# A hybrid decoder layer on one core: two expert weight loads wait for the row gathers, router logits with three copies of the columns, identity products on TensorE

## The reference

```python
h2 = rms_norm(x, ln2_g[l]) * (1.0 + scale2) + shift2
x = x + gate2 * hierarchical_moe(h2, w_rg[l], b_rg[l], w_re[l], b_re[l], w1[l], w3[l], w2[l])

def hierarchical_moe(h, w_rg, b_rg, w_re, b_re, w1, w3, w2):      # cut
    p_group = jax.nn.softmax(ht @ w_rg + b_rg)
    pg_top, g_idx = lax.top_k(p_group, 1)
    e_logits = (ht @ w_re + b_re).reshape(T, N_GROUPS, EXPERTS_PER_GROUP)
    e_logits = jnp.take_along_axis(e_logits, g_idx[:, :, None], axis=1)[:, 0]
    pe_top, e_idx = lax.top_k(jax.nn.softmax(e_logits), 2)
    weights = pg_top * pe_top / jnp.sum(pe_top, axis=-1, keepdims=True)
    ...
    hid = jax.nn.silu(lax.ragged_dot(xs, w1, sizes)) * lax.ragged_dot(xs, w3, sizes)
    ys = lax.ragged_dot(hid, w2, sizes) * weights[order][:, None]
    out = jax.ops.segment_sum(ys, tok, num_segments=T)
```

## Time and profile before

| | |
|---|---|
| median of 3 runs | 1135.82 us (1133.02 to 1141.98) |
| the profiled execution, its own time | 1136.39 us |
| its span in the profile | 1134.6 us |
| TensorE busy | 1037.5 us (91%) |
| VectorE, ScalarE, GpSimd busy | 49%, 30%, 13% |
| read from HBM, over the span | 271.99 MB, 243 GB/s with the writes |

### The profile page before, as it was taken

How to read it: one execution, slowest core, us unless ns; L and a number is a source line. 1 busy time by engine, 2 the same in 40 slices (tenths; PEclk the granted TensorE clock), 3 DMA queues, 4 the chain that set the end, 5 groups by cost and what they waited for, 6 DMA issues and landing times.

```text
span 1134.6 us, 19418 instructions
## 1 busy us (share of the span) xinstructions
PE 1037.5 (91%) x8496; PEld 686.1 (60%) x8496; DVE 556.7 (49%) x883; ACT 335.2 (30%) x567; POOL 149.4 (13%) x168
## 2 busy tenths in 40 slices
PE   4799999899998889999996599999999998999998
PEld 3567799798995668878786234444444443444443
DVE  4548861534536857575565333333333332333334
ACT  6367753032326762322322011111111111111110
POOL 0000000360894430000000100000000000000000
PEclk9899999998989989999997599999999999999999
DMA  9431121000004046566648599999999999999993
GB/s 365 150 149 56 60 90 38 14 5 4 4 3 149 7 148 206 185 215 212 223 167 334 199 380 406 404 396 408 401 408 412 411 417 403 414 413 410 421 419 131
DMA packets 44917, 273.26 MB, mean 241 GB/s; under 512 B 7408, under 2 KB 7552, under 8 KB 31008
## 3 DMA queue, kind: packets, MB, share of 16 engines
q1 hardware_dynamic: 41168, 264.42, 59.2%
q0 software_dynamic: 2656, 4.28, 1.3%
q10 hardware_dynamic: 1008, 3.31, 0.7%
HBM read 271.99 MB, written 4.19 MB: 243 GB/s over the span
## 4 chain that ended last, share of the span: by engine, by line
PE 68%; DMA 20%; DVE 7%; ACT 3%; issue 2%; SPq 0%; ACTq 0%; DVEq 0%; POOLq 0%
PE banks L1543 26%; DMA w_qkv<-in_w 17%; PE banks L1978 13%; PE banks L1992 6%; PE banks L2012 2%; PE banks L1694 2%; DMA tokm<-in_w_ada 2%; PE banks L1971 1%; PE banks L1696 1%; PE banks L1709 1%; PE banks L2013 1%; PE banks L1836 1%; DMA picked<-h_table,slot_rows 1%; PE banks L1984 1%; PE banks L1922 1%
## 5 line engine op out<-in xcount | busy, mean ns | idle before, releaser
L1978 PE MATMUL banks<-w_ring,xT 128*64 128x512 f32 x336 | 147.8, 593 | 8.5 <-DMA w_ring<-in_w 4.3
L1471 DVE TENSOR_TENSOR hid<-banks,silu_a 64x512 f32<-64x512 f32 x32 | 22.2, 693 | 197.4 <-ACT silu_a L841 197.4
L1978 PEld LDWEIGHTS banks<-w_ring,xT 128*64 128x64 f32 x336 | 45.2, 137 | 103.2 <-issue 103.2
L841 ACT ACTIVATE silu_a<-banks 64x512 f32<-64x512 f32 x32 | 18.9, 591 | 276.0 <-PE banks L1979 276.0
L1459 DVE SCALAR_TENSOR_TENSOR mod<-banks,row_weight,mod 64x512 f32<-64x512 f32 x64 | 47.9, 748 | 93.2 <-PE banks L1992 92.2
L930 POOL DMA_INDIRECT picked<-h_table,slot_rows x32 | 30.2, 944 | 468.2 <-PE banks L1971 398.3
L1978 PE MATMUL banks<-w_ab,xT 128*64 128x512 f32 x176 | 81.8, 620 | 6.1 <-DMA w_tok<-in_w 5.3
L1465 DVE TENSOR_TENSOR x<-x,banks 128x512 f32<-128x512 f32 x120 | 77.1, 684 | 18.7 <-PE banks L2013 18.3
L1992 PE MATMUL banks<-w_ring,hidT 128*64 128x512 f32 x352 | 82.1, 609 | 1.0 <-ACT hidT L845 1.0
L1979 PE MATMUL banks<-w_tok,xT 128*64 128x512 f32 x176 | 81.9, 621 | 0.0
L1979 PE MATMUL banks<-w_ring,xT 128*64 128x512 f32 x176 | 77.6, 594 | 0.0
(11 more groups left out here) (368 smaller groups left out, 2359.3 us busy)
## 6 DMA issues: line engine op xcount, KB each, us to landing
w_ring<-in_w SPq DMA_DIRECT2D x54, 2048.0 KB, 32.6
w_tok<-in_w SPq DMA_DIRECT2D x21, 2048.0 KB, 35.1
w_ab<-in_w SPq DMA_DIRECT2D x11, 2048.0 KB, 30.2
w_qkv<-in_w SPq DMA_DIRECT2D x10, 2048.0 KB, 35.9
ada_buf<-in_w_ada SPq DMA_DIRECT2D x64, 256.0 KB, 3.5
tokm<-in_w_gate SPq DMA_DIRECT2D x3, 2048.0 KB, 14.0
ring<-in_w_mix SPq DMA_DIRECT2D x5, 1024.0 KB, 4.7
ring<-in_w_ada SPq DMA_DIRECT2D x2, 2048.0 KB, 14.2
```

The source lines that it names most:

```text
L1978: pe.matmul(bank[2][0:SLOTS, :], xT[:, b, k, :], w1[:, k, :], start=(k == 0), stop=(k == KT - 1))
```

## The change

Three edits. (1) On SyncE, w3 of expert 2, and with it w2 of expert 2 and all that stands behind, waits for the landing of the first two gathers instead of for the stores of h2 (the gathers themselves still wait for the stores). (2) Each logits product reads the 36 router columns three times, through a step of zero, and writes 108 columns; VectorE reads the first copy of each. (3) TensorE multiplies the identity by four copies of itself, 128x512 in float32, into bank 5, which nobody reads: once after the logits of tile 0, nine times before the wait for the picks, twice before the wait for the slots, five times before the wait for the first gather.

```diff
@@ load_w13 @@
                 if e == 2:
-                    sp.wait_ge(h2_stored, 16 * TT)
+                    for b in range(2):
+                        sp.wait_ge(rows_in[b], 16)
                     sp.wait_ge(h2t_mm, KT)
                 sp.dma_start(W3_IN[c], w3_src[e]).then_inc(w3_in[c], 16)
@@ vector @@
-            seq(dve.tensor_tensor(L, bank[0][:, 0:TT * NR].rearrange("p (t n) -> p t n", n=NR),
+            seq(dve.tensor_tensor(L, bank[0][:, 0:3 * TT * NR].rearrange("p (t c n) -> p t c n", t=TT, c=3)[:, :, 0, :],
                                   b_route.unsqueeze(1).to_broadcast([P, TT, NR]), ALU.add))
@@ tensor @@
+            thrice = bank[0][:, 0:3 * TT * NR].rearrange("p (t c n) -> p t c n", t=TT, c=3)
+
+            def keep_running(n):
+                for _ in range(n):
+                    pe.matmul(bank[5][:, :].rearrange("p (a n) -> p a n", a=4), ident, ident.unsqueeze(1).to_broadcast([P, 4, P]), start=True, stop=True)
...
-                    mm = pe.matmul(bank[0][:, NR * t:NR * t + NR], h2T[:, k, P * t:P * t + P], w_route[:, k, :], start=(k == 0), stop=(k == KT - 1))
+                    mm = pe.matmul(thrice[:, t, :, :], h2T[:, k, P * t:P * t + P], w_route[:, k, :].unsqueeze(1).to_broadcast([P, 3, NR]),
+                                   start=(k == 0), stop=(k == KT - 1))
...
             turn_h2(1)
             logits(0)
+            keep_running(1)
             turn_h2(2)
             logits(1)
             logits(2)
             turn_h2(3)
             logits(3).then_inc(logit_mm, 1)
+            keep_running(9)
             pe.wait_ge(picks_v, 1)
...
             mm.then_inc(rank_mm, 1)
+            keep_running(2)
...
             fill_table(bank[4][0:SLOTS, 0:2 * NEXP], values.rearrange("p j c n -> p j (c n)"))
+            keep_running(5)
```

## The result

The changed kernel takes 1132.02 us (median of 20 runs, 1126.61 to 1135.42), the kernel before 1138.88 us (median of 20 runs that include the three shown above, 1133.02 to 1142.98). The ratio is 0.9945, with a 95% interval of 0.993 to 0.996: 4.5 to 8 us faster, a small gain and a sure one. The forecast was 1126.2 with a range up to 1131.5; the time lies 0.5 us above the range and 5.8 above the forecast.

What follows compares the result with a forecast made beforehand. The prediction took the DMA engines to bound the expert stage: loads starting 20.6 us earlier, less 11.0 for transfers put off, gain 9.6. From the profiled 1136.39 that gives 1126.8, less 0.6 to the median 1126.2; range 1121.5 to 1131.5.

Steps and rivals of the forecast that it cites:

- w3 of expert 2 at 632.1: On SyncE's queue: this load goes out at about 632.1 us, behind both gathers, and starts the unbroken loads.
- The fourth store as the floor: Before the first gather: the fourth store of h2_table lands at 626.4, after the row numbers at 625.9, and decides.
- the clock held to the table: TensorE's router: at full clock logits end 3.5 us earlier, the table takes about 1.1 us, row numbers come at 625.9.
- gathers of some 3.2 us: First two gathers: with the two loads behind them, each lands in 3.2 us instead of 8.8 to 9.8.
- the price of a load put off: Expert stage: each load moved into busy DMA time costs 5.1 to 5.3 us; two loads and a gather 11.0.
- The TensorE rival: End of kernel: TensorE ends it, so its whole shift of 13.2 us counts, giving 1122.6 us; chance 0.14.
- the five weight transfers in the chain: Expert stage from 853 to 1079 us: five transfers of 38 to 40 us with hardly anything between, read as DMA-bound.
- it is issued at 652.69: SyncE's queue before the change: w1 of expert 3 goes out at 652.69 us, and from there the queue never empties.
- 652.69 − 632.1 − 11.0: Net gain: start of unbroken loads moves 20.6 us earlier, less 11.0 for two loads and a gather: 9.6 us.
- the clock falls: Rival, during the logits: TensorE drops to half clock anyway, row numbers are not earlier, gain 5.6 us, about 1130.2; chance 0.14.
- The rival that blocks the router with dense products at half clock: TensorE's queue: products at 1.71 us each delay the router, w1 of expert 3 goes 10.5 us later, 1146; chance 0.04.
- The gathers are slow for another reason: Rival, first gathers: not the 4 MB slows them, they land in 9.8 us again, net 3.1 us, 1132.7; chance 0.04.

Runs made afterwards that it cites:

- e7: The changed kernel with w1 of expert 2 also waiting for both first gathers, so three first loads wait: ratio 0.9972 to the kernel before.
- e8: The changed kernel with w1 and w3 of expert 8 loading only 16 of 4096 columns each, output not the layer's: ratio 0.9861 to the kernel before.
- e1: The kernel before with only the first edit, the wait for the first two gathers; logits and router unchanged: ratio 0.9948 to the kernel before.
- e2: The changed kernel with the old wait for the stores back, so only the copies and dense products remain: ratio 0.9994 to the kernel before.
- e3: The changed kernel with 36 columns in the logits again, keeping the wait and dense products: ratio 0.9934 to the kernel before.
- e4: The changed kernel without the dense products, keeping the wait and the three copies: ratio 0.9946 to the kernel before.
- e6: The changed kernel with w3 of expert 2 waiting for the first gather only, and w1 of expert 2 for the four stores: ratio 0.9961 to before.

## Why the prediction was wrong

The time of 1132.02 is 5.8 us above the forecast. 3.1 of them are the median of before: it was 1135.82 of three runs and is 1138.88 of twenty. The other 2.7 are the gain, 6.9 by the medians in place of 9.6 (6.3 by the ratio).

**Right: what the changed kernel does.** w3 of expert 2 at 632.1 is +30.7; measured +30.8, +31.0, +30.9. The fourth store as the floor (0.7 us later than forecast), the clock held to the table, three copies at no cost, nine products just short of the picks, gathers of some 3.2 us: all as written. The up products ran at half clock for 3.4 us and w1 of expert 3 went out at +40.7, +41.0 and +40.7, not +38.1. The prediction had allowed for +40.6; the second of the two loads in front of it landed only at +44.5 to +44.9, so no gap opened. The last landing was to move from 1113.4 by 9.6, to +502.4; it came at +503.05, +505.0 and +503.8, on average 1.5 us later.

**Right: the bound and the price of a load put off.** e7 (one load more in the unbroken stretch, 3.2 us longer than the mean of the changed kernel though the loads start 1.4 earlier) and e8 (two loads less, 9.2 us off the same mean) give 4.6 us a load, a little under the 5.1 to 5.3 of the prediction and within what single profiles can tell. The TensorE rival had 0.14 and is refuted. One reading was loose: the five weight transfers in the chain do not follow one another with hardly anything between. Each begins 7.7 us after the end of the one before (853.45 + 38.12 = 891.57, the next at 899.31). That the DMA engines are the bound rests on their share of 1.01 and on e7 and e8.

**Wrong: the step "it is issued at 652.69", taken as the state of the kernel before.** The net was 652.69 − 632.1 − 11.0. 652.69 is +51.3, and it stood there because the clock had fallen in the logits of that one execution. I priced "the clock falls" only as a rival for the changed kernel and never asked whether it always falls in the kernel before. In three of four profiles it does not; then w1 of expert 3 goes out at +45.8, and the same sum gives 45.8 − 30.8 − 11.0 = 4.0 us, and the stretches show 529.1 − 525.1 = 4.0. That they agree so closely is in part luck: w1 of expert 3 went out 5.5 us earlier, the stretch got only 4.1 us shorter, and repeats of one kernel differ by 1.3 to 2.0 us. Of the 5.6 us between 9.6 and 4.0, then, 4.1 are the state of the kernel before (533.2 against 529.1), and 1.5 are the changed kernel's end, which came that much later than forecast. With one execution in four like the profiled one the sum gives 0.75 x 4.0 + 0.25 x 9.6 = 5.4 us, and the mean stretches of all four and all three profiles give 530.1 − 525.1 = 5.0; both are inside the measured 4.5 to 8. One in four is a count of four profiles and no more; in e1 the clock fell in both.

**So what of the change pays.** In an execution whose clock holds, the gather starts when it did before and takes 3.4 instead of 9.2 us; expert 0, and with it the unbroken loads, come earlier. That is the wait's doing, and e1 with the wait alone has the ratio of the whole change. No profile of e1 with the clock held came up, so for that state this rests on its ratio. Its two profiled executions took 1133.42 and 1135.47 us, against a median of 1129.98 over its twelve runs. e2 shows that TensorE's edits alone gain nothing that can be measured. Shown for one execution each: without the copies (e3) or without the products (e4) the stretch is that of the changed kernel, and their ratios do not differ from its ratio. What they may be good for together is that the clock never fell in the logits, in twelve profiles, against three of six; the one product that e3 keeps between the tiles held it once. How much that is worth over many runs stays open: the ratios of e1 (0.9948) and of the changed kernel (0.9945) do not differ.

**The other rivals.** The clock did not fall in the logits in any of the three profiles of the changed kernel. The rival that blocks the router with dense products at half clock did not occur either. "The gathers are slow for another reason" fell: the first two took 2.8 to 3.8 us in the ten profiles in which the two loads waited and w1 of expert 2 was through, at most half a microsecond after the start of the first gather, or waited as well (e7).

## What to carry to other kernels

Where transfers are the bound for good from some moment on, a change in front of it is worth the shift of that moment less the transfers that it puts off: move small urgent transfers ahead of large ones that nobody needs yet, and count what is put off at full price. Before a stall in a single profile is sold as a gain, take more profiles: a stretch that depends on the clock can be there in one execution and not in the next. And compare from a common event in both profiles, since the first 600 us of the same code differed here by 4.5 us.

## What I had not expected of the hardware

The granted clock of the same instructions at the same place differs between executions: for the logits of the kernel before 3.66 us at 2.4 GHz in one, 5.40 us with the fall to 1.2 GHz inside in another. A gather of 256 KB beside a single 2 MB load in another queue took 7.4 us in e6, and 3.4 without one in the changed kernel. The fourth store of 512 KB, issued at +11.5 in one profile of before and at +8.9 in another, landed at +25.1 and +25.0: the one ahead of it in its queue had landed at +19.0 and +18.9 only.
